# Attention rows of a decoder kernel: both heads scaled on VectorE instead of one on VectorE and one on GpSimd

## The chip, the cores and the metric

One core of a Trainium2 chip runs the whole program. The metric is the device time of one execution in microseconds (us). Before the change the median of 3 runs is 932.4 us (927.18 to 932.52).

## What is computed

One layer of a decoder is run for a prompt of 512 tokens and, with the same weights, for 8 sample sequences of one token each. The part that matters here is the attention of the prompt over its own tokens (selected-block and sliding-window branches). With 512 tokens both branches see all earlier tokens, so each is a causal softmax, and the results are mixed by sigmoid gates:

```python
s_s = jnp.einsum('bqhgd,bhqksd->bhgqks', qg, gk, preferred_element_type=f32) * scale
p_s = masked_softmax(s_s.reshape(sh[:4] + (-1,)), m_s.reshape(...)).reshape(sh)
o_s = jnp.einsum('bhgqks,bhqksd->bqhgd', p_s, gv.astype(f32))
s_w = jnp.einsum('bqhgd,bkhd->bhgqk', qg, kw, preferred_element_type=f32) * scale
p_w = masked_softmax(s_w, (dlt >= 0) & (dlt < WINDOW) & (kpos >= 0)[None, :])
o_w = jnp.einsum('bhgqk,bkhd->bqhgd', p_w, vw.astype(f32))
gt = jax.nn.sigmoid(g.astype(f32)).reshape(B, Tq, NSA_KV_HEADS, NSA_GROUP, 3)
o = gt[..., 0:1] * o_c + gt[..., 1:2] * o_s + gt[..., 2:3] * o_w
```

Everything is fp32. The compressed branch `o_c`, the mLSTM and pool groups, the output projection, the FFN and the samples' own attention belong to the program too; the change touches none of them.

## The kernel before

The kernel has one instruction stream per engine, with semaphores between them that are written out by hand. Its stages run in this order: norms and the input projection (N_IN tiles of weights), mLSTM, the attention loop, the output projection and the FFN. In the dense stages each weight tile is split into a high and a low part: ScalarE writes the high part (line 1043), GpSimd the low part (line 641), TensorE multiplies with both (line 687).

The attention loop works on 32 units, `UNITS = [(hq, i, r) ...]` (line 415): 4 head indices `hq`, for each 4 query blocks `i` of 128 tokens, for each 2 branches `r` (0 selected, 1 window). One unit handles the two heads `hq` and `hq + 4` at once, as `g = 0` and `g = 1`. A unit of query block `i` has rows of (i + 1) x 128 keys, so its width is 128, 256, 384 or 512 per head, and each width comes twice in a row. Eight units make one `hq`. Below, u0 to u7 are the units of one `hq`: u0 and u1 have width 128, u6 and u7 width 512.

For unit k the engines do this:

- TensorE, `scores(k)` (line 907): the scores of both heads into banks 2(k % 2) and the next one. It waits for `p_exp` of unit k - 2, which frees the banks.
- VectorE: adds the causal mask (line 1675) and takes the negative maximum (line 1676, `mx_ready`).
- ScalarE: exponentials with the row sum, once per head (line 1246, `p_exp`), into `pr[k % 3]`.
- VectorE, one iteration later (lines 1684 to 1689): the reciprocal of the sums, times the gate, gives `fac`, one factor for each head. `fac_ready` tells GpSimd. VectorE then multiplies head g = 0's rows by its factor (line 1688, `p_ready`).
- GpSimd (lines 632 to 636): waits for `fac_ready`, multiplies head g = 1's rows by its factor (line 635), and signals `p_pool`.
- TensorE, `flip(k)` three iterations later (line 922): waits for `p_ready` and `p_pool`, and for the copy of the unit before (`pt_act`), then transposes the rows into banks 4 and 5. For r = 0 it also transposes the compressed branch's rows (line 927).
- ScalarE copies the transposed rows to SBUF (line 1239, `pt_act`). VectorE copies the compressed branch's (line 1695, `pt_dve`, r = 0 only).
- TensorE, `values(k)` four iterations later (lines 940 and 943): products with V. For r = 0 it waits for `pt_dve`, and when also i is 0 or 2 it first does `sample_values` (line 957), the value products of one sample sequence, for which that sequence's rows must have come by DMA.
- VectorE evacuates the result (lines 1705 and 1706, after r = 1 units).

TensorE's order within iteration k is `scores(k)`, `flip(k - 3)`, `values(k - 4)`. VectorE's order within iteration k is mask and maximum of unit k, factor and scaling of unit k - 1, the copy for unit k - 3, the evacuation of unit k - 5. Since `fac` has two slots, VectorE waits before it writes the slot of unit v until `p_pool` shows that GpSimd has read it for unit v - 2 (line 1683).

The value rows of the sample sequences are issued meanwhile by SyncE, one page at a time (line 490, 16 per sequence), and one window load per sequence (line 494). GpSimd's part of the loop stands in its program between the second and the third low part of the output weights' tiles; the third waits for a high part that ScalarE makes after the loop.

Of the kernel before, what the change touches and what calls it, by code (L numbers as in the profile page):

```python
# [16 lines left out]
ALU = mybir.AluOpType  # L17
# [3 lines left out]
P = 128  # L21
# [25 lines left out]
N_IN = 21  # L47
# [117 lines left out]
def trunk_kernel(nc, xT, wst, par_d, con_d, hot_d, ltri_d, pt_d, cacheA, cacheV, winK, winV, mC, mst, plst, ffst,  # L165
                 o_y, o_fm, o_vn, o_st, o_snv, o_wk, o_wv, o_C, o_m, o_pool, o_sC, o_sn, o_sm, o_spool, o_ffp, o_ffs):
    with ExitStack() as ctx:
# [3 lines left out]
        def sem(name):  # L171
            return ctx.enter_context(nc.semaphore(name))
# [60 lines left out]
        sn, gN, cout, smr, cst = lay(27464, [1152, 96, 260, 214, 1024])  # L233
        gN = gN.rearrange("p (i n) -> p i n", i=ST)
# [17 lines left out]
        pr = [pr2[:, 0], pr2[:, 1], md.rearrange("p (r n) -> p r n", r=2)]  # L252
# [34 lines left out]
        fac = sb("fac", [P, 2, 2])  # L287
# [76 lines left out]
        csc_done, pcx_ready, pcx_exp, pc_ready = sem("csc_done"), sem("pcx_ready"), sem("pcx_exp"), sem("pc_ready")  # L364
        qk_done, mx_ready, p_exp, p_ready, t_done = sem("qk_done"), sem("mx_ready"), sem("p_exp"), sem("p_ready"), sem("t_done")
        pt_act, pt_dve, pv_done, o_evac = sem("pt_act"), sem("pt_dve"), sem("pv_done"), sem("o_evac")
        fac_ready, p_pool = sem("fac_ready"), sem("p_pool")
        cout_ready = sem("cout_ready")
        pool_ready, pool_mm, side_mix = sem("pool_ready"), sem("pool_mm"), sem("side_mix")
        snew_done, wsc_done, wsc_evac, sgate_moved, sg_exp = (sem("snew_done"), sem("wsc_done"), sem("wsc_evac"),  # L370
# [44 lines left out]
        UNITS = [(hq, i, r) for hq in range(G) for i in range(ST) for r in range(2)]  # L415
# [150 lines left out]
        def _(pool):  # L566
# [59 lines left out]
            for i, g in enumerate(SPLIT):  # L626
                if i == N_IN:
                    pool.wait_ge(con_landed, 16)
                    pool.wait_ge(rec_landed, 32)
                    pool.wait_ge(mmix_ready, 1)  # L630
                    pool_heads()
                if i == N_IN + 2:
                    for v, (hq, b, r) in enumerate(UNITS):
                        pool.wait_ge(fac_ready, v + 1)
                        nc.gpsimd.tensor_scalar(pr[v % 3][:, 1, 0:(b + 1) * P], pr[v % 3][:, 1, 0:(b + 1) * P], fac[:, v % 2, 1:2], None, ALU.mult)\  # L635
                            .then_inc(p_pool, 1)
                if i == 3 or (7 <= i < N_IN):
                    value_products(half)
                    half += 1
                pool.wait_ge(hi_ready, i + 1)  # L640
                nc.gpsimd.tensor_tensor(wR[:, i % 2, 1, :, :], raw[:, g % RAW, :, :], wR[:, i % 2, 0, :, :].bitcast(F32),  # L641
                                        ALU.subtract).then_inc(lo_ready, 1)
# [3 lines left out]
        def _(pe):  # L646
# [141 lines left out]
            for t in range(2):  # L788
                for i in range(ST):
                    last = nc.tensor.transpose(ps[:, 4 + t, i * P:(i + 1) * P], pT[:, T_MK + t, i * P:(i + 1) * P], ident)  # L790
            last.then_inc(kn_T, 1)
            for c, t in enumerate([T_MQ, T_MQ + 1, T_MK, T_MK + 1, T_G]):
                last = nc.tensor.transpose(ps[0:NB, c // 4, (c % 4) * P:(c % 4 + 1) * P], sT[:, t, :], ident)
            last.then_inc(sn_T, 1)
            for i in range(ST):
                last = nc.tensor.transpose(ps[:, 3, i * P:(i + 1) * P], pT[:, T_G, i * P:(i + 1) * P], ident)
# [18 lines left out]
            for c in range(4 * ST):  # L815
                if c in (0, 8):
                    window_scores(c // 8)
                r, i = c // ST, c % ST
                at = (c % 8) * 2 * NCP
                last = mm(ps[:, r // 2, at:at + 2 * NCP], pT[:, r, i * P:(i + 1) * P], kct[:, 64:64 + 2 * NCP],  # L820
                          start=True, stop=True)
# [89 lines left out]
            def flip(u):  # L911
                hq, i, r = UNITS[u]
                pe.wait_ge(p_ready, u + 1)
                pe.wait_ge(p_pool, u + 1)
                if u == 0:
                    pe.wait_ge(pc_ready, 1)
                    pe.wait_ge(side_mix, 1)
                else:
                    pe.wait_ge(pt_act, u)
                for g in range(2):  # L920
                    for c in range(i + 1):
                        last = nc.tensor.transpose(ps[:, 4 + g, c * P:(c + 1) * P], pr[u % 3][:, g, c * P:(c + 1) * P], ident)  # L922
                if r == 0:
                    if u >= 4:
                        pe.wait_ge(o_evac, u // 2 - 1)
                    for g in range(2):
                        last = nc.tensor.transpose(ps[0:NCP, 6 + u // 2 % 2, 256 + g * P:256 + (g + 1) * P],  # L927
                                                   pc[:, (hq + G * g) * ST + i, 0:NCP], ident)
                last.then_inc(t_done, 1)
# [394 lines left out]
        def _(dve):  # L1324
# [3 lines left out]
            def link(ins):  # L1328

                chain[0] += 1  # L1330
                ins.then_inc(dve_step, 1)
                dve.wait_ge(dve_step, chain[0])
# [336 lines left out]
            for k in range(NU + 5):  # L1669
                if k < NU:  # L1670
                    hq, i, r = UNITS[k]
                    two = ps[:, 2 * (k % 2):2 * (k % 2) + 2, :]
                    dve.wait_ge(qk_done, k + 1)
                    d = two[:, :, i * P:(i + 1) * P]
                    link(V.tensor_tensor(d, d, con_("cq").unsqueeze(1).broadcast_to([P, 2, P]), ALU.add))
                    V.tensor_reduce(nmx[:, k % 2, :], two[:, :, 0:(i + 1) * P], AX, ALU.max, negate=True).then_inc(mx_ready, 1)  # L1676
                if 1 <= k <= NU:
                    v = k - 1
                    hq, i, r = UNITS[v]
                    a = v % 2  # L1680
                    dve.wait_ge(p_exp, v + 1)
                    if v >= 2:
                        dve.wait_ge(p_pool, v - 1)
                    link(V.reciprocal(fac[:, a, :], sm[:, a, :]))
                    V.tensor_tensor(fac[:, a, :], fac[:, a, :], gN[:, i, 3 * hq + 1 + r:3 * hq + 14 + r:12], ALU.mult)\  # L1685
                        .then_inc(fac_ready, 1)
                    dve.wait_ge(fac_ready, v + 1)
                    V.tensor_scalar(pr[v % 3][:, 0, 0:(i + 1) * P], pr[v % 3][:, 0, 0:(i + 1) * P], fac[:, a, 0:1], None, ALU.mult)\
                        .then_inc(p_ready, 1)
                if 3 <= k < NU + 3 and not UNITS[k - 3][2]:  # L1690
                    v = k - 3
                    dve.wait_ge(t_done, v + 1)
                    if v >= 2:
                        dve.wait_ge(pv_done, v - 1)
                    V.tensor_copy(pcT[0:NCP, :, :], ps[0:NCP, 6 + v // 2 % 2, 256:256 + 2 * P].rearrange("p (g n) -> p g n", g=2))\
                        .then_inc(pt_dve, 1)
                if k >= 5 and UNITS[k - 5][2]:
                    v = k - 5
                    hq, i, r = UNITS[v]
                    bank = 6 + v // 2 % 2  # L1700
                    dve.wait_ge(pv_done, v + 1)
                    if i % 2 == 0:
                        b = 2 * hq + i // 2
                        dve.wait_ge(spv_done, b + 1)
                        V.tensor_copy(so8[:, b * P:(b + 1) * P], ps[:, bank, P:2 * P])
                    V.tensor_copy(mix[:, hq, i * P:(i + 1) * P], ps[:, bank, 0:P]).then_inc(o_evac, 1)
# [245 lines left out]
```

## Time and profile before

| | us |
|---|---|
| median of 3 runs | 932.4 |
| lowest and highest run | 927.18, 932.52 |
| the profiled execution: its own time | 932.81 |
| the profiled execution: span, first to last instruction | 931.0 |
| TensorE busy in the span | 845.6 |
| VectorE busy | 494.6 |
| ScalarE busy | 348.5 |
| GpSimd busy | 337.8 |

The mean granted clock of TensorE is 0.905 of full speed. The attention loop begins at about 355 us of the span and its last evacuation is at 461.5 us. "Busy" counts only instructions that compute. PE is TensorE's matmuls, PEld its weight loads, DVE VectorE, ACT ScalarE, POOL GpSimd, SPq the DMA issues of SyncE.

### The profile page before, as it was taken

Reading aid. Unit: us, or ns where it says so; the run is one execution under the profiler, and the core shown is the slowest. Engines: PE = TensorE matmul, PEld = TensorE weight load, DVE = VectorE, ACT = ScalarE, POOL = GpSimd, SP = SyncE. Lnnn points to the kernel's source line nnn. Section 1 sums busy time; section 2 is a strip of 40 time slices with the busy share of each in tenths; the row PEclk is TensorE's granted clock in tenths of the full one; section 3 lists DMA queues with packets and bytes.
Section 4 is the critical chain, followed back from the end, with each engine's and each line's share of the span. In section 5 each row is a group of like instructions: output and inputs, shape, how many; then the busy total and the mean of one; then the engine's idle time right before and its main releaser. Section 6 shows DMA issues by size and latency. Waiting matters only on the chain.

```text
span 931.0 us, 19070 instructions
## 1 busy us (share of the span) xinstructions
PE 845.6 (91%) x7555; PEld 750.2 (81%) x7555; DVE 494.6 (53%) x938; ACT 348.5 (37%) x675; POOL 337.8 (36%) x204
## 2 busy tenths in 40 slices
PE   4669999998998688899899699999999999999994
PEld 3458999987556564566699599999999999999994
DVE  0061456565435985667547756666621366667224
ACT  2432222233322133656432355555311355554321
POOL 0133455451000584434324134444344444443440
PEclk9869999999555655999989899999999999999998
DMA  9732788883105772445026123434322333222222
GB/s 346 289 131 73 221 265 261 270 261 129 35 13 179 283 269 41 105 116 154 8 79 254 46 80 114 114 113 115 102 92 91 106 113 121 93 92 90 92 63 92
DMA packets 72438, 128.28 MB, mean 138 GB/s; under 512 B 13652, under 2 KB 48156, under 8 KB 72096
## 3 DMA queue, kind: packets, MB, share of 16 engines
q1 hardware_dynamic: 65664, 109.65, 36.9%
q10 hardware_dynamic: 6656, 17.43, 5.6%
q8 instruction: 60, 0.98, 0.5%
q14 instruction: 26, 0.21, 0.1%
q0 software_dynamic: 32, 0.00, 0.0%
HBM read 121.39 MB, written 9.11 MB: 140 GB/s over the span
## 4 chain that ended last, share of the span: by engine, by line
PE 73%; DVE 13%; SPq 7%; issue 2%; ACT 2%; DMA 1%; POOL 0%; DVEq 0%; ACTq 0%; POOLq 0%
PE ps L687 56%; SPq L490 2%; PE ps L855 2%; PE ps L870 2%; SPq L429 2%; PE ps L744 2%; PE ps L943 1%; PE ps L922 1%; PE ps L907 1%; DVE sq L1354 1%; PE ps L957 1%; SPq L516 1%; DMA arena<-cache_keys 1%; PE ps L737 1%; DVE hR L1362 1%
## 5 line engine op out<-in xcount | busy, mean ns | idle before, releaser
L687 PE MATMUL ps<-hR,wR 128*128 128x260 f32 x3504 | 436.4, 286 | 21.7 <-ACT hR L1051 17.8
L687 PEld LDWEIGHTS ps<-hR,wR 128*128 128x128 f32 x3504 | 429.9, 191 | 27.1 <-issue 19.3
L641 POOL TENSOR_TENSOR wR<-raw,wR 128x1024 fp32r<-128x1024 f32 x95 | 227.7, 2397 | 321.8 <-ACT wR L1043 321.8
L1043 ACT ACTIVATE wR<-raw 128x1024 fp32r<-128x1024 f32 x95 | 100.4, 1058 | 217.8 <-PE ps L687 214.2
L687 PE MATMUL ps<-fR,wR 128*128 128x260 f32 x1056 | 128.1, 283 | 2.2 <-DVE fR L1746 2.0
L687 PEld LDWEIGHTS ps<-fR,wR 128*128 128x128 f32 x1056 | 127.0, 188 | 3.1 <-DVE fR L1746 2.4
L1768 DVE COPY arena<-arena 128x2 f32<-128x2 f32 x44 | 47.1, 1071 | 94.1 <-ACT arena L1301 94.1
L578 POOL TENSOR_TENSOR arena<-arena,par 128x1024 f32<-128x1024 f32 x16 | 33.4, 2089 | 89.8 <-DMA arena<-cache_keys 89.8
L1372 DVE TENSOR_REDUCE arena<-arena 128x64 f32<-128x1024 f32 x16 | 19.5, 1219 | 86.0 <-POOL arena L578 86.0
L1731 DVE TENSOR_TENSOR t<-ps,mod 128x8 f32<-128x8 f32 x24 | 4.0, 166 | 108.8 <-PE ps L687 108.8
L635 POOL TENSOR_SCALAR arena<-arena,fac 128x128 f32<-128x128 f32 (+3 forms) x32 | 40.7, 1274 | 57.2 <-DVE fac L1685 57.1
L1246 ACT ACTIVATE arena<-ps,nmx 128x128 f32<-128x128 f32 (+3 forms) x64 | 33.2, 526 | 13.5 <-DVE nmx L1676 12.8
L1773 DVE SCALAR_TENSOR_TENSOR arena<-arena,par 128x512 f32<-128x512 f32 x44 | 37.1, 844 | 1.6
L1301 ACT ACTIVATE arena<-arena,par 128x520 f32<-128x520 f32 x44 | 36.2, 823 | 1.5
L1239 ACT ACTIVATE arena<-ps 128x256 f32<-128x256 f32 (+3 forms) x32 | 22.5, 704 | 36.0 <-PE ps L927 29.5
L594 POOL MEMSET arena<- 128x15 f32 x2 | 0.2, 110 | 97.5 <-DVE arena L1575 97.5
L1375 DVE TENSOR_TENSOR arena<-arena,par 128x1024 f32<-128x1024 f32 x16 | 35.2, 2202 | 0.0
L1772 DVE SCALAR_TENSOR_TENSOR arena<-arena,par 128x512 f32<-128x512 f32 x44 | 33.1, 752 | 1.6
L907 PE MATMUL ps<-arena 64*128 64x128 f32 (+3 forms) x128 | 27.8, 519 | 3.3 <-ACT arena L1246 3.3
L922 PEld LDWEIGHTS ps<-con,arena 128*128 128x128 f32 x160 | 17.4, 144 | 16.3 <-issue 11.3
L1298 ACT ACTIVATE arena<-ps 128x520 f32<-128x520 f32 x44 | 25.8, 587 | 6.7 <-DVE fR L1746 6.7
L1025 ACT ACTIVATE sq<-x 128x520 f32<-128x520 f32 x22 | 13.9, 638 | 36.8 <-DVE x L1735 28.7
(334 smaller groups left out, 994.6 us busy)
## 6 DMA issues: line engine op xcount, KB each, us to landing
raw<-weights SPq DMA_DIRECT2D x95, 512.0 KB, 3.8
arena<-cache_keys SPq DMA_DIRECT2D x128, 192.0 KB, 3.3
arena<-weights SPq DMA_DIRECT2D x24, 512.0 KB, 10.5
arena<-cache_values SPq DMA_DIRECT2D x128, 64.0 KB, 1.9
arena<-weights ACTq DMA_DIRECT2D x12, 512.0 KB, 5.6
raw<-weights ACTq DMA_DIRECT2D x12, 512.0 KB, 4.8
x<-xT SPq DMA_DIRECT2D x8, 260.0 KB, 6.3
out_y<-x SPq DMA_DIRECT2D x8, 260.0 KB, 2.2
```

The costliest lines, as they stand in the source:

```text
L578: nc.gpsimd.tensor_tensor(tmpv.rearrange("p (a n j) -> p a n j", a=HALF, j=16), pages[:, s, :, 2 * P:3 * P].rearrange("p a (n j) -> p a n ...
L635: nc.gpsimd.tensor_scalar(pr[v % 3][:, 1, 0:(b + 1) * P], pr[v % 3][:, 1, 0:(b + 1) * P], fac[:, v % 2, 1:2], None, ALU.mult)\
L641: nc.gpsimd.tensor_tensor(wR[:, i % 2, 1, :, :], raw[:, g % RAW, :, :], wR[:, i % 2, 0, :, :].bitcast(F32), ALU.subtract).then_inc(lo_read ...
L687: last = mm(ps[:, a + half, 0:TH], wR[:, i % 2, wp, k, :], src[:, hp, j, half * TH:(half + 1) * TH], start=(j == 0 and q == 0), stop=(j == ...
L907: last = mm(ps[:, 2 * (u % 2) + g, 0:n], pT[hr[g], hq, i * P:(i + 1) * P], pT[hr[g], t, 0:n], start=True, stop=True)
L1043: A(wR[:, i % 2, 0, :, :], raw[:, g % RAW, :, :], ACT.Identity).then_inc(hi_ready, 1)
L1246: last = A(pr[k % 3][:, g, 0:n], ps[:, 2 * (k % 2) + g, 0:n], ACT.Exp, bias=nmx[:, k % 2, g:g + 1], accum_out=sm[:, k % 2, g:g + 1])
L1301: A(yab[:, b, :], zb[:, b, 2:T + 2], ACT.Identity, bias=par_("conv_b", t, t + 1), scale=par_("conv_w", 3 * t + 2, 3 * t + 3)).then_inc(y_r ...
L1375: link(V.tensor_tensor(v, v, par_("wpos", 48, 64).unsqueeze(1).unsqueeze(1).broadcast_to([P, HALF, 8, 16]), ALU.mult))
L1768: V.tensor_copy(ffo_p[:, t, :], z[:, S:S + 2])
L1772: link(V.scalar_tensor_tensor(y[:, 0:S], z[:, 1:S + 1], w[1], y[:, 0:S], ALU.mult, ALU.add))
L1773: last = V.scalar_tensor_tensor(y[:, 0:S], z[:, 0:S], w[0], y[:, 0:S], ALU.mult, ALU.add)
```

## The change

GpSimd's multiply of head g = 1 goes. VectorE multiplies both heads' rows, one after the other, and signals `p_ready` with the second. The semaphores `fac_ready` and `p_pool` are gone, with the wait of TensorE in `flip` and the wait of VectorE before it writes `fac`. The wait of VectorE between the factor and the scaling stays, as a link on its own semaphore.

```diff
@@ GpSimd
-                if i == N_IN + 2:
-                    for v, (hq, b, r) in enumerate(UNITS):
-                        pool.wait_ge(fac_ready, v + 1)
-                        nc.gpsimd.tensor_scalar(pr[v % 3][:, 1, 0:(b + 1) * P], pr[v % 3][:, 1, 0:(b + 1) * P], fac[:, v % 2, 1:2], None, ALU.mult)\
-                            .then_inc(p_pool, 1)
@@ TensorE, flip(u)
                 pe.wait_ge(p_ready, u + 1)
-                pe.wait_ge(p_pool, u + 1)
@@ VectorE
                     dve.wait_ge(p_exp, v + 1)
-                    if v >= 2:
-                        dve.wait_ge(p_pool, v - 1)
                     link(V.reciprocal(fac[:, a, :], sm[:, a, :]))
-                    V.tensor_tensor(fac[:, a, :], fac[:, a, :], gN[:, i, 3 * hq + 1 + r:3 * hq + 14 + r:12], ALU.mult)\
-                        .then_inc(fac_ready, 1)
-                    dve.wait_ge(fac_ready, v + 1)
-                    V.tensor_scalar(pr[v % 3][:, 0, 0:(i + 1) * P], pr[v % 3][:, 0, 0:(i + 1) * P], fac[:, a, 0:1], None, ALU.mult)\
-                        .then_inc(p_ready, 1)
+                    link(V.tensor_tensor(fac[:, a, :], fac[:, a, :], gN[:, i, 3 * hq + 1 + r:3 * hq + 14 + r:12], ALU.mult))
+                    for g in range(2):
+                        last = V.tensor_scalar(pr[v % 3][:, g, 0:(i + 1) * P], pr[v % 3][:, g, 0:(i + 1) * P], fac[:, a, g:g + 1],
+                                               None, ALU.mult)
+                    last.then_inc(p_ready, 1)
```

## Rows read from the trace of the kernel before

**Rows 1.** The page: the chain that ended last, share of the span by engine

```profile
PE 73%; DVE 13%; SPq 7%; issue 2%; ACT 2%; DMA 1%; POOL 0%; DVEq 0%; ACTq 0%; POOLq 0%
```

**Rows 2.** Busy time of each engine in stretches of the loop: stretch, length, engines, clock

```profile
355.00:394.60 39.60, 33.17 (x298) 20.40 (x297) 26.66 (x77) 19.67 (x62) 16.24 (x14) 0.82 0.41 79
...
417.57:440.91 23.34, 22.99 (x271) 15.10 (x269) 17.19 (x50) 14.23 (x40) 10.23 (x9) 1.00 0.51 145
```

**Rows 3.** Waits from 354 to 465 us: in total, times, longest

```profile
POOL arena L635 <- DVE fac L1685: 57.1, 28, 5.7
...
DVE ps L1675 <- PE ps L907: 24.7, 19, 4.6
...
PE ps L957 <- DMA arena<-win_values: 3.0, 1, 3.0
```

**Rows 4.** Groups by shape from 354 to 465 us: the scaling instructions

```profile
L635 POOL TENSOR_SCALAR arena<-arena,fac 128x512 f32<-128x512 f32 x8 | 14.7, 1842 | 5.1 <-DVE fac L1685 5.0
...
L1688 DVE TENSOR_SCALAR arena<-arena,fac 128x512 f32<-128x512 f32 x8 | 4.0, 498 | 0.3
...
L1688 DVE TENSOR_SCALAR arena<-arena,fac 128x384 f32<-128x384 f32 x8 | 3.4, 420 | 0.3
...
L1688 DVE TENSOR_SCALAR arena<-arena,fac 128x256 f32<-128x256 f32 x8 | 2.8, 353 | 0.3
...
L1688 DVE TENSOR_SCALAR arena<-arena,fac 128x128 f32<-128x128 f32 x8 | 2.3, 287 | 0.3
```

**Rows 5.** Timeline, third hq, VectorE: start, duration, instruction, idle before it

```profile
421.40 0.43 DVE L1675 TENSOR_TENSOR ps<-ps,con 128x256 f32<-128x256 f32 x1 [1.44 <-PE ps L907]
...
423.12 0.42 DVE L1688 TENSOR_SCALAR arena<-arena,fac 128x384 f32<-128x384 f32 x1
423.46 0.41 DVE L1695 COPY pcT<-ps 31x256 f32<-31x256 f32 x1
...
425.77 0.42 DVE L1688 TENSOR_SCALAR arena<-arena,fac 128x384 f32<-128x384 f32 x1
426.10 0.28 DVE L1705 COPY arena<-ps 128x128 f32<-128x128 f32 x1
...
428.48 0.49 DVE L1688 TENSOR_SCALAR arena<-arena,fac 128x512 f32<-128x512 f32 x1
428.88 0.41 DVE L1695 COPY pcT<-ps 31x256 f32<-31x256 f32 x1
...
432.84 0.43 DVE L1675 TENSOR_TENSOR ps<-ps,con 128x256 f32<-128x256 f32 x1 [1.76 <-PE ps L907]
```

**Rows 6.** Timeline, second and third hq: TensorE around sample_values, ScalarE's last exponential of u6

```profile
406.05 1.30 PE L957 MATMUL ps<-arena 128*32 128x128 f32 x40 [0.35 <-DVE pcT L1695]
...
426.18 0.68 ACT L1246 ACTIVATE arena<-ps,nmx 128x512 f32<-128x512 f32 x1
...
428.19 0.84 PE L922 MATMUL ps<-con,arena 128*128 128x128 f32 x6
429.39 0.38 PE L957 MATMUL ps<-arena 128*32 128x128 f32 x5 [0.35 <-issue]
```

**Rows 7.** Timeline, GpSimd's pair of scalings and VectorE's scaling inside it

```profile
428.54 3.77 POOL L635 TENSOR_SCALAR arena<-arena,fac 128x512 f32<-128x512 f32 x2 [1.24 <-DVE fac L1685]
...
430.39 0.49 DVE L1688 TENSOR_SCALAR arena<-arena,fac 128x512 f32<-128x512 f32 x1
```

**Rows 8.** Timeline, first hq: sample_values, and the window load that it waits for

```profile
379.68 1.30 PE L957 MATMUL ps<-arena 128*32 128x128 f32 x40 [0.21 <-issue]
...
391.51 0.43 SPq L494 DMA_DIRECT2D arena<-win_values  x1
...
394.62 1.30 PE L957 MATMUL ps<-arena 128*32 128x128 f32 x40 [2.99 <-DMA arena<-win_values]
```

**Rows 9.** Timeline, SyncE: window loads of the second and third hq

```profile
402.81 0.43 SPq L494 DMA_DIRECT2D arena<-win_values  x1
...
425.30 0.44 SPq L494 DMA_DIRECT2D arena<-win_values  x1
```

More of the change, by code:

```diff
@@ L366, in trunk_kernel @@
         pt_act, pt_dve, pv_done, o_evac = sem("pt_act"), sem("pt_dve"), sem("pv_done"), sem("o_evac")
-        fac_ready, p_pool = sem("fac_ready"), sem("p_pool")
         cout_ready = sem("cout_ready")
```

## Prediction, written before the changed kernel was run

> **What bounds the kernel now.** I read the page's chain of waits first. TensorE makes up 73% of the chain that ended last, VectorE 13%, GpSimd 0% [rows 1]. So the GpSimd work that the change removes is on no path that sets the end. The only stretch touched is the attention loop, from about 355 to 461.5 us. The table of stretches comes next [rows 2]. In the third hq, 417.57 to 440.91, TensorE is busy for 22.99 of 23.34 us at full clock (granted 1.00, the 2.4 GHz level), VectorE for 17.19, ScalarE for 14.23, GpSimd for 10.23. There the loop is bound by TensorE, with 0.35 us left over. In the first stretch, 355.00 to 394.60, TensorE is busy for 33.17 of 39.60 us, so something else is late.
>
> Then the waits [rows 3]. GpSimd waits for VectorE's factor, 57.1 us in total, and no row shows anybody waiting for GpSimd's scaling. VectorE's scaling has no matmul waiting for it either; where weight loads are put down to it, they overlap with matmuls in flight. VectorE has 24.7 us of idle time before its mask additions, waiting for scores, in 19 of the 32 units. In the other 13 units it doesn't wait: there it is behind. That is where added work can hurt, so the last view is the timeline of one such place.
>
> In the third hq VectorE waits for the last time at 421.40 [rows 5] (mask of u5) and then runs without a break until after 430 us. In between lies its copy for u4, 428.88 to 429.29, and TensorE needs it: its transposes end at 429.03 (428.19 + 0.84), and `sample_values` starts at 429.39 after 0.35 us of nothing [rows 6]. The trace calls that wait "issue"; at the same place of the second hq, 406.05, it names the copy, line 1695, with the same 0.35 us [rows 6]. So once per hq VectorE sets TensorE's pace, at the copy for u4, and it already does so by 0.35 us. The 0.10 us from the copy's end to the matmul is the hand-over. The fourth hq repeats the pattern. VectorE catches up right after: it waits 1.76 us at 432.84 [rows 5], during `sample_values`.
>
> **The change, part by part.**
>
> *GpSimd's 32 multiplies and its hand-overs go.* GpSimd's multiply of a 512-wide row takes 1.84 us [rows 4], from 0.06 us after VectorE's own start. Even the pair that begins at 428.54 is over at 432.31 (428.54 + 3.77) [rows 7], and the transposes that need it come later, since TensorE starts the flip of a unit two iterations after its scaling. Gain on the path: 0. The wait of VectorE for `p_pool` (line 1683) and that of TensorE (line 914) are satisfied when they are reached; their removal is worth nothing visible, from 0 to a few hundredths of a microsecond each, and TensorE's is covered by matmuls in flight. After the loop GpSimd's next instruction waits for a high part that ScalarE makes only then, so it starts no earlier. No DMA and no queue of SyncE is moved.
>
> *VectorE's link.* The wait after the factor existed before (on `fac_ready`); now it is on VectorE's own semaphore. Cost 0.
>
> *VectorE's second multiply.* 32 instructions are added: 8 of each width. Their durations in the kernel before are 0.498, 0.420, 0.353 and 0.287 us [rows 4], 12.5 us in all (8 x 1.558). What one costs VectorE is less, because the next instruction starts before it has ended: from line 1688's start to the next start there are 0.34 us (384 wide, 423.12 to 423.46), 0.33 us (384, 425.77 to 426.10) and 0.40 us (512, 428.48 to 428.88) [rows 5]. Two multiplies in a row don't occur before. The lower bound of one is 0, if it vanished in a wait; the upper bound is the whole duration. I take the distance from start to start, since it is measured on the same instruction.
>
> Most of them are hidden. Of the eight masks of an hq, five have idle time before them (19 waits in 32 units, 24.7 us, 1.3 us each on average [rows 3]); the scalings of u7, u0, u1, u2 and u3 come right ahead of these five, and the added multiply goes into that idle time. What isn't hidden is what lies between the mask of u5 (421.40) and the copy for u4 (428.88): the scalings of u4, u5 and u6, of widths 384, 384 and 512. The copy moves by 0.34 + 0.33 + 0.40 = 1.07 us. TensorE is already waiting there, so `sample_values` moves by the same 1.07 us. A smaller effect lies before it: the copy for u2 at 423.46 moves by 0.34 and delays TensorE by about 0.2 us, but this is part of the same 1.07, since TensorE then only waits less later. The scaling of u7 comes behind the copy and falls into the 1.76 us before 432.84.
>
> Does anything absorb it? What `sample_values` also waits for is the window load. Its load is issued at 402.81 and 425.30 for the second and third hq [rows 9]; the load issued at 391.51 is the one that TensorE waited for, and TensorE starts at 394.62, so such a load takes about 3.0 us [rows 8]. So they land at 405.8 and 428.3, before the copy's end (about 405.95, a hand-over ahead of 406.05, and 429.29), and SyncE's order doesn't depend on VectorE: no absorption. In the first hq it is otherwise. The place is at 379.68, with 0.21 us of wait, and the delay there can be at most 1.07 us. But then TensorE comes to the next `sample_values` and waits 2.99 us for a window load that SyncE could not issue before 391.51, busy as it is with page loads [rows 8]. A delay up to 2.99 us vanishes there. So three of four count: 3 x 1.07 = 3.2 us.
>
> What is late next: with a TensorE wait of 0.35 + 1.07 = 1.4 us per hq, ScalarE's exponentials of u6 move by 0.34 us too. They end at 426.86 now (426.18 + 0.68), and what waits for them are the scores of the next u0, short matmuls just ahead of the transposes at 428.19 [rows 6]; about 0.8 us of room is left, and they stay hidden.
>
> *A rule against the change.* The rows give a scaling of 512 a cost of 0.40 us and one of 384 0.33 us [rows 5]. The Trainium skill, VectorE: DVE Perf Modes, section on the TRN2 errata, says that an SBUF to SBUF instruction pays a fixed 58 cycles besides its elements, so that two short instructions pay it twice where one long one pays it once. By that formula, with two elements a cycle, the three would cost about 0.27 + 0.27 + 0.33 = 0.87 us, an estimate from the page, and the sum would be 2.6 us instead of 3.2. The rows are taken instead.
>
> The sum is made against the profiled execution: 932.81 + 3.2 = 936.0 us. That execution lies 0.4 us above the median of the runs, so against the median I expect 932.4 + 3.2 = 935.6 us, 0.34% more.
>
> **The rivals.**
>
> *Everything exposed (slower by over 1%).* VectorE becomes the bound of the whole loop, not of three units in eight. The place is the mask addition, the price the whole 12.5 us of added duration, the time 932.4 + 12.5 = 944.9. For it: VectorE's 17.19 us per hq become 20.3 (plus 2 x 1.558), and hand-overs between its linked instructions aren't counted as busy. Against it: 24.7 us of idle time before the masks [rows 3], which is twice the added work, and 5 of the 8 units of an hq have such idle time. It decides from the point where the copy of u4 comes so late that VectorE no longer has any wait before 432.84; that needs 1.76 us more than now and 0.4 us at most is added there. Chance 0.07.
>
> *Nothing is exposed.* The second multiply flows behind the first, or the load of the window is what TensorE waits for after all. The margins of 0.2 and 1.0 us between landing and copy, worked out above, are small enough that a load landing 1 us later in another run would swallow the delay. Time 932.4. Chance 0.20.
>
> *VectorE gains from GpSimd's silence.* If the two engines hinder each other at the SBUF, VectorE's instructions get shorter once GpSimd is quiet. Against it: VectorE's scaling at 430.39 runs wholly inside GpSimd's pair and takes 0.49 us, as does the one at 428.48 that starts before GpSimd does [rows 5, 7]. The price would have to come from the rest of VectorE's run from 421.40 to 429.29; if each of its instructions in it were 5% shorter, that is 0.4 us per hq, 1.2 us in all, and the time would be 934.4, or 931.2 where the multiply is hidden too. Chance 0.06. The Trainium skill, GPSIMD Engine Reference, section Key points, says that GpSimd shares its SBUF interfaces with VectorE and that they contend with a VectorE instruction that uses both ports or has two SBUF inputs, which speaks for this rival; the two equal durations speak against its size here.
>
> *The change doesn't do what it says.* A wait that remains (for `p_exp`, `pt_act`) could hold both multiplies where they were. That is the case of no exposure, and is counted there.
>
> **How the numbers follow.** Forecast 0.67, everything exposed 0.07, nothing exposed 0.20, GpSimd's silence 0.06. About 1% is what a measurement of this kernel can tell from no change. The bounds of the unknown cost are 0 and the full durations, 4 x (0.420 + 0.420 + 0.498) = 5.4 us, so 932.4 to 937.8. The runs of the kernel before spread downward by 5 us, which a median of few runs can inherit in part: low end 930.5. The upper end takes in a part of the way to the first rival: 940. Slower by over 1% is above 941.7: 0.07. Faster by over 1% is below 923.1; no case reaches it, and I leave 0.02 for what I haven't seen. The rest, 0.91, is within 1%.
>
> **What would show it.** Right: in the changed trace TensorE waits some 1.4 us before line 957 in the second, third and fourth hq, for line 1695; an hq of the later ones takes 24.4 instead of 23.34 us; the wait for the window load in the first hq shrinks from 2.99 to about 2.2 us, and its end stays at 394.6; two multiplies in a row start 0.33 to 0.41 us apart at widths 384 and 512; VectorE's idle time before its masks falls but doesn't vanish. Wrong: an hq of 23.34 us as before (nothing exposed), or no idle time before the masks and waits of TensorE in most units (everything exposed), or line 1688's instructions shorter than 0.42 and 0.498 us (GpSimd's silence).

## The result and the profile after

The changed kernel takes 933.68 us (median of 20 runs, 930.87 to 938.68), the kernel before 931.85 us (median of 20 runs, 926.64 to 935.92). The ratio is 1.0034, with a 95% interval of 1.0021 to 1.0047: 2.0 to 4.4 us slower, 3.2 us in the middle. The two medians by themselves differ by only 1.8 us, the two means by 3.0 us. The prediction was 935.6 us, a change of +3.2 us or 0.34%.

The page of the changed kernel: busy time of the engines, and the chain that ended last.

```profile
PE 844.9 (91%) x7555; PEld 749.1 (80%) x7555; DVE 501.4 (54%) x970; ACT 348.9 (37%) x675; POOL 297.9 (32%) x172
...
PE 73%; DVE 14%; SPq 7%; issue 2%; ACT 2%; DMA 1%; POOL 0%; DVEq 0%; ACTq 0%; POOLq 0%
```

GpSimd lost 39.9 us of work (337.8 to 297.9), none of which was on the chain [rows 1]. VectorE's share of the chain rose from 13 to 14%. The span of this one execution is 930.7 us, even 0.3 us under that of the kernel before. The timed runs say otherwise; why this one execution doesn't show the cost comes below.

The timeline of VectorE in the third hq of the changed kernel: start, duration, instruction, idle before it. Line 1668 is the mask (1675 before), 1678 the scaling (1688), 1686 the copy (1695), 1696 the first evacuation (1705).

```profile
419.62 0.43 DVE L1668 TENSOR_TENSOR ps<-ps,con 128x256 f32<-128x256 f32 x1 [1.17 <-PE ps L901]
...
421.35 0.75 DVE L1678 TENSOR_SCALAR arena<-arena,fac 128x384 f32<-128x384 f32 x2
422.01 0.41 DVE L1686 COPY pcT<-ps 31x256 f32<-31x256 f32 x1
...
424.32 0.75 DVE L1678 TENSOR_SCALAR arena<-arena,fac 128x384 f32<-128x384 f32 x2
424.99 0.28 DVE L1696 COPY arena<-ps 128x128 f32<-128x128 f32 x1
...
427.37 0.88 DVE L1678 TENSOR_SCALAR arena<-arena,fac 128x512 f32<-128x512 f32 x2
428.17 0.41 DVE L1686 COPY pcT<-ps 31x256 f32<-31x256 f32 x1
...
432.13 0.43 DVE L1668 TENSOR_TENSOR ps<-ps,con 128x256 f32<-128x256 f32 x1 [1.37 <-PE ps L901]
```

From the mask of u5 to the copy for u4 it is 8.55 us (419.62 to 428.17), where it was 7.48 us (421.40 to 428.88) [rows 5]: 1.07 us more. The pairs take 0.66, 0.67 and 0.80 us from start to the next start, twice what one took to within 0.02 us. The idle time before the mask at the other end fell from 1.76 to 1.37 us.

TensorE's first matmul of `sample_values` (line 950, before 957) in the changed kernel, from the first to the third hq, with the idle time before it.

```profile
379.68 1.30 PE L950 MATMUL ps<-arena 128*32 128x128 f32 x40 [0.91 <-issue]
...
391.79 1.30 PE L950 MATMUL ps<-arena 128*32 128x128 f32 x40 [0.16 <-DMA arena<-win_values]
...
404.28 1.30 PE L950 MATMUL ps<-arena 128*32 128x128 f32 x40 [0.91 <-issue]
...
416.16 1.30 PE L950 MATMUL ps<-arena 128*32 128x128 f32 x40
...
428.68 1.30 PE L950 MATMUL ps<-arena 128*32 128x128 f32 x40 [0.91 <-issue]
...
440.56 1.30 PE L950 MATMUL ps<-arena 128*32 128x128 f32 x40
```

This gives the yardstick for all that follows. Call the distance from an hq's first `sample_values` to its second the first interval, and from there to the next hq's the second. In the changed kernel the first interval is 12.49 us (391.79 to 404.28) and 12.52 us (416.16 to 428.68); before it was 11.43 us (394.62 to 406.05 [rows 6, 8]) and 11.46 us (417.93 to 429.39). The second interval is 11.88 us, as before. So each hq pays 1.06 us, all of it in the first interval. Inside one execution these intervals repeat to a few hundredths of a microsecond wherever no window load is late and the granted clock is 1.00, while whole runs spread over 8 us.

The waits of the changed kernel from 371 to 465 us (in total, times, longest) say where TensorE spends it.

```profile
PE ps L950 <- issue: 3.7, 4, 0.9
...
PEld ps L920 <- DVE arena L1697: 0.9, 3, 0.3
...
PE ps L933 <- DVE pcT L1686: 0.5, 3, 0.2
```

Three places share the loss. `sample_values` waits 0.91 us, where it waited 0.35 before. The values of u2 (line 933) wait 0.17 us for VectorE's copy. And the weight load of the transposes of u4's compressed rows (line 920) waits 0.3 us for line 1697, the evacuation of u1. From start to start of TensorE's work these are 0.56, 0.23 and 0.26 us more than before, together the 1.06 us; the prediction put them all in one place.

Why does the profiled execution not show 3.2 us? SyncE's page loads. The timeline of SyncE in the changed kernel:

```profile
365.30 23.31 SPq L489 DMA_DIRECT2D arena<-cache_values  x32
388.65 0.44 SPq L493 DMA_DIRECT2D arena<-win_values  x1
```

and in the kernel before:

```profile
366.04 25.43 SPq L490 DMA_DIRECT2D arena<-cache_values  x32
```

The same 32 issues took 2.1 us less, and began 0.7 us earlier. So the window load that held TensorE until 394.62 before [rows 8] landed 2.8 us earlier here, and TensorE reached it almost when it had landed (0.16 us of wait). That is a difference between executions: in two other kernels of this study with the same SyncE program, a_copy_first and third_slack, the 32 issues took 23.1 and 25.1 us. From the second hq on, the changed trace loses three times 1.06 us against that of before: from the first `sample_values` of the second hq to the last one it is 61.29 us (391.79 to 453.08), and 58.11 us before (394.62 to 452.73). By that point it is 0.35 us behind; what makes the whole span 0.3 us shorter lies after the loop.

### The profile page after: what moved, and what is told of

Read it like the earlier page. It is cut to its first block, busy times and chain, and to the rows that moved or that the text cites. A ratio compares the mean times of both kernels' runs of the same rounds, so it can differ in the third digit from the quotient of the medians.

```text
span 930.7 us, 19039 instructions
## 1 busy us (share of the span) xinstructions
PE 844.9 (91%) x7555; PEld 749.1 (80%) x7555; DVE 501.4 (54%) x970; ACT 348.9 (37%) x675; POOL 297.9 (32%) x172
## 4 chain that ended last, share of the span: by engine, by line
PE 73%; DVE 14%; SPq 7%; issue 2%; ACT 2%; DMA 1%; POOL 0%; DVEq 0%; ACTq 0%; POOLq 0%
PE ps L681 56%; PE ps L849 2%; PE ps L864 2%; SPq L489 2%; SPq L428 2%; PE ps L738 2%; PE ps L936 1%; DVE sq L1347 1%; PE ps L950 1%; SPq L515 1%; PE ps L915 1%; DMA arena<-cache_keys 1%; PE ps L731 1%; PE ps L901 1%; DVE hR L1355 1%
## 5 line engine op out<-in xcount | busy, mean ns | idle before, releaser
L1368 DVE TENSOR_TENSOR arena<-arena,par 128x1024 f32<-128x1024 f32 x16 | 32.8, 2050 | 0.0
L1669 DVE TENSOR_REDUCE nmx<-ps 128x2 f32<-128x256 f32 (+3 forms) x32 | 26.4, 825 | 1.1
```

The costliest lines, as they stand in the source:

```text
L1368: link(V.tensor_tensor(v, v, par_("wpos", 48, 64).unsqueeze(1).unsqueeze(1).broadcast_to([P, HALF, 8, 16]), ALU.mult))
```

## The experiments

**Which of the 32 multiplies cost.** Two kernels divide them. `ONPOOL` lists the units whose head g = 1 stays on GpSimd, with `fac_ready` and `p_pool` for these units alone:

```diff
+        ONPOOL = [v for v in range(len(UNITS)) if v % 8 in (4, 5, 6)]        # wide_on_pool
+        ONPOOL = [v for v in range(len(UNITS)) if v % 8 not in (4, 5, 6)]    # rest_on_pool
...
-                    for g in range(2):
+                    for g in range(1 if v in ONPOOL else 2):
```

> The changed kernel, but head g = 1 of units u4, u5 and u6 of each hq (widths 384, 384, 512) is scaled on GpSimd again; the other 20 units stay on VectorE. Theory (only what lies between the mask of u5 and the copy for u4 counts): from the first to the second sample_values of the second, third and fourth hq 11.4 us as in the kernel before (12.5 in the changed one), TensorE's wait there 0.35 us; time that of the kernel before, 0 +- 1 us, so about 3 us under the changed kernel. Rival (every added multiply costs a little): 20 of 32 multiplies stay, some 1.5 to 2 us of the 3.2 stay, spread over the whole hq, with intervals of 11.7 or more and over 11.95 for the other half.

> The complement: GpSimd scales head g = 1 of u0 to u3 and u7, VectorE both heads of u4, u5 and u6 only. Theory: 12.5 us from the first to the second sample_values as in the changed kernel, other half 11.95; the full 3.2 us over the kernel before. Rival (every multiply counts, or GpSimd's absence gives something back): 1.2 to 1.7 us over the kernel before.

TensorE's `sample_values` in the third hq, first of wide_on_pool:

```profile
412.86 1.30 PE L960 MATMUL ps<-arena 128*32 128x128 f32 x40
...
424.31 1.30 PE L960 MATMUL ps<-arena 128*32 128x128 f32 x40 [0.35 <-DVE pcT L1703]
```

then of rest_on_pool:

```profile
413.22 1.30 PE L960 MATMUL ps<-arena 128*32 128x128 f32 x40
...
425.73 1.30 PE L960 MATMUL ps<-arena 128*32 128x128 f32 x40 [0.91 <-issue]
```

11.45 us with 0.35 us of wait, and 12.51 us with 0.91: the kernel before and the changed kernel, to 0.01 us. The fourth hq agrees (11.43 and 12.52 us). In wide_on_pool's second hq it is 11.58 us, with 0.49 us of wait for a window load. Twelve multiplies carry the whole interval, the other twenty nothing. The times agree: 1.0015 of the kernel before (0.999 to 1.004) and 1.0042 (1.0017 to 1.0067). The first of them can't be told from 1 or from 1.0034 by itself; the intervals in the traces decide.

**More VectorE work, inside the run and outside.** Two kernels add a third multiply, by 1.0, which changes no value:

```diff
+                    if v % 8 in (7, 0, 1, 2, 3):        # third_slack;  third_run: (4, 5, 6)
+                        link(last)
+                        last = V.tensor_scalar(pr[v % 3][:, 1, 0:(i + 1) * P], pr[v % 3][:, 1, 0:(i + 1) * P], con_("ones", 0, 1), None, ALU.mult)
```

> The changed kernel with a third multiply (by 1.0, in place on head g = 1, behind the second, with a wait between) on VectorE in units u7, u0, u1, u2 and u3 of each hq. Added VectorE work start to start about 0.52 + 2 x 0.3 + 2 x 0.38 = 1.9 us per hq, 7.5 us in all. Theory (there is idle time ahead of those masks): intervals 12.5 and 11.95 us as before, at most 0.3 us more per hq where u2's slack of 0.3 us is used up; total 0 to 1 us. Rival (everything VectorE does counts): 1.9 us more per hq, up to 7.5 us in all.

> The changed kernel with a third multiply (by 1.0, in place on head g = 1, behind the second with a wait between) in units u4, u5 and u6 only, between the mask of u5 and the copy for u4. Added start to start: the link lets the second end (0.42 - 0.33 and 0.49 - 0.40, plus 0.04 each), then the third 0.33, 0.33 and 0.40: 0.46 + 0.46 + 0.53 = 1.45 us. Theory: interval 12.5 + 1.45 = 13.9 to 14.0 us, other half 11.9, 4.4 us over the changed kernel from three hqs and up to 5.8 with the first. Compare third_slack, where more VectorE work elsewhere brought 0.18 us per hq. Rival (the chain is not that of VectorE): less than 1 us per hq.

TensorE's `sample_values` in the third hq of third_slack:

```profile
417.34 1.30 PE L950 MATMUL ps<-arena 128*32 128x128 f32 x40
...
429.83 1.30 PE L950 MATMUL ps<-arena 128*32 128x128 f32 x40 [0.91 <-issue]
```

and of third_run:

```profile
420.06 1.30 PE L950 MATMUL ps<-arena 128*32 128x128 f32 x40
...
434.00 1.25 PE L950 MATMUL ps<-arena 128*32 128x128 f32 x37 [1.43 <-issue]
```

The first stays at 12.49 us; its second interval is 12.06 us instead of 11.88 (405.28 to 417.34), so about 1.9 us of added work costs 0.18 us per hq. The second goes to 13.94 us in the third and in the fourth hq, 1.42 us more for an expected 1.45 us of added work. In time: 1.0040 (1.0011 to 1.0069) and, from six runs, 1.0072 (1.0046 to 1.0098).

The second hq of third_run doesn't fit: 16.00 us (392.18 to 408.18). There TensorE had waited 2.09 us for the window load, and behind it the granted clock was 0.50, the lower of TensorE's two levels (1.2 GHz), for some 6 us. Stretch, length, busy time of TensorE, its weight loads, VectorE, ScalarE and GpSimd, then the granted clock:

```profile
394.00:400.00 6.00, 6.00 (x28) 3.03 (x30) 2.45 (x7) 1.13 (x4) 0.00 (x0) 0.50 0.35 97
```

In the kernel before a wait of 2.99 us at the same place left the clock at 1.00, so why it fell here stays open. This execution took 939.92 us, the longest of the six.

**The place of the copy.** The copy for unit k - 3 goes ahead of the factor and scaling of unit k - 1, in both kernels:

```diff
+                if 3 <= k < NU + 3 and not UNITS[k - 3][2]:
...
+                    V.tensor_copy(pcT[0:NCP, :, :], ...).then_inc(pt_dve, 1)
                 if 1 <= k <= NU:
...
-                if 3 <= k < NU + 3 and not UNITS[k - 3][2]:
...
```

> The changed kernel with VectorE's copy for unit k - 3 placed ahead of factor and scaling of unit k - 1 instead of behind them. Theory (the copy for u4 is late because the scaling stands before it): the copy starts 1.2 us earlier (0.19 + 0.19 + 0.40 + 0.40), TensorE's wait before sample_values goes from 0.91 to about 0, the first interval falls from 12.5 to 11.1 to 11.3 us, the time falls by 3.5 to 4 us against the changed kernel, to 0.5 to 1 us under the kernel before. Rival (VectorE's throughput is what bounds the stretch, not the place of the copy): the wait moves to another place, the scores or the transposes, and the interval stays over 12 us.

> The kernel before with the same move of the copy. Theory: the 0.35 us of TensorE's wait before sample_values vanish, the first interval falls from 11.4 to 11.1 us, the time by 1.0 us (three times 0.35). Rival (that wait is the hand-over itself or something else than the copy): 0.35 us stay.

TensorE in the third hq of a_copy_first:

```profile
414.47 1.30 PE L950 MATMUL ps<-arena 128*32 128x128 f32 x40
...
423.83 0.41 PE L920 MATMUL ps<-con,arena 128*31 128x128 f32 x2 [0.31 <-DVE arena L1697]
...
426.00 1.30 PE L950 MATMUL ps<-arena 128*32 128x128 f32 x40
```

The wait before `sample_values` is gone and the interval falls from 12.5 to 11.53 us, less than the expected 11.1 to 11.3: 0.31 us are left at another thing that stands behind the scalings, the evacuation of u1, for which the transposes of u4's compressed rows wait. So the rival, a wait that moves to another place, holds for a small part. The time is 1.0000 of the kernel before (0.998 to 1.002): within that interval, the order of VectorE's instructions wins back the cost of the change.

TensorE in b_copy_first, third hq and start of the fourth:

```profile
412.78 1.30 PE L957 MATMUL ps<-arena 128*32 128x128 f32 x40
...
423.91 1.30 PE L957 MATMUL ps<-arena 128*32 128x128 f32 x40
...
436.47 1.30 PE L957 MATMUL ps<-arena 128*32 128x128 f32 x40 [0.61 <-DMA arena<-win_values]
```

11.13 us, as expected, but TensorE then waits 0.61 us at the next window load. The time, 0.9986 (0.9967 to 1.0006), isn't clear of 1. Against this kernel, which has the copy in the same place, a_copy_first is still 0.40 us slower per hq (11.53 against 11.13 us): the new order doesn't make the added multiplies free.

**What absorbed the first hq's delay.** The window load of sequence 2 is put ahead of the page loads of sequence 3, in both kernels:

```diff
             load_values(2)
+            sp.wait_ge(spv_done, 1)
+            load_window(2)
             load_values(3)
             for b in range(2, NB):
-                sp.wait_ge(spv_done, b - 1)
-                load_window(b)
+                if b > 2:
+                    sp.wait_ge(spv_done, b - 1)
+                    load_window(b)
```

> The changed kernel with the window load of sample sequence 2 issued ahead of the page loads of sequence 3 instead of behind them. Theory (what absorbs the first hq's delay is this load's issue): the wait of TensorE for the window at the beginning of the second hq goes; that sample_values begins at about 391.6 us in all executions, whatever SyncE's page loads take. In traces where the load was late (before: by 2.99 us) this is a gain up to 3 us, in the changed kernel's own trace it was late by 0.16 only. Time 0 to 2 us under the changed kernel. Rival (the load itself or the pages are late): the wait stays or names the pages.

> The kernel before with the same early window load. Theory: without that wait the first hq's delay would count too, so the distance to a_win_early grows from 3.2 to 3.9 us (0.91 - 0.21 = 0.7 more); the second hq's first sample_values begins at about 390.9 us; time 1 to 3 us under the kernel before. Rival (the first hq never had a share): distance 3.2.

In a_win_early, TensorE's `sample_values` of sequence 3 and the window load that it needs:

```profile
399.75 0.43 SPq L493 DMA_DIRECT2D arena<-win_values  x1
...
402.76 1.30 PE L953 MATMUL ps<-arena 128*32 128x128 f32 x40 [1.50 <-ACT arena L1235]
```

and the same matmul in b_win_early:

```profile
402.61 1.30 PE L960 MATMUL ps<-arena 128*32 128x128 f32 x40 [2.12 <-DMA arena<-win_values]
```

The wait at sequence 2 went (its `sample_values` begins at 389.66 and 389.38 us without a wait), and a new one came at sequence 3, in both kernels at the same time, 402.6 to 402.8 us. The trace of a_win_early names ScalarE, but the copy that TensorE needs from it there, that of u4, had ended at 400.27 us; the load was issued at 399.75, and with the 3.0 us that such a load takes to land it is there at about 402.75. So my theory was too narrow. What holds TensorE is not that one load but SyncE's rate: 16 page loads and a window load take it 10 to 14 us with what stands between them, nearly what TensorE needs for one sequence. With the load moved, the delays of the first and of the second hq both vanish in SyncE's lateness, and two hqs are left that count. The traces show these two: from sequence 3 to the last `sample_values` it is 48.79 us in a_win_early and 46.68 us in b_win_early, 2.11 us or 2 x 1.06 apart. The times are 1.0005 (0.9982 to 1.0028) and 0.9978 (0.9959 to 0.9998) of the kernel before; their distance, 0.27% or 2.5 us, is near it, but with intervals of this width it can't exclude the 3.9 us that I had expected.

The trace of a_win_early also shows that the first hq is a case of its own. From 363 to 371 us the granted clock was 1.00 in it, and 0.50 in the traces of before and after. With TensorE that much faster VectorE is further behind: TensorE waits 1.50 us for the copy for u2 and 1.38 us before `sample_values`, where the changed kernel's trace has no wait and 0.91 us.

The window loads can also leave SyncE altogether, since GpSimd is idle in the loop of the changed kernel (this queue counts on semaphores of its own, `vwin_soft`; the edit on SyncE, which drops `load_window` from its loop, and the one on TensorE, which waits for `vwin_soft`, are left out here):

```diff
+                if i == N_IN + 2:
+                    for b in range(2, NB):
+                        pool.wait_ge(spv_done, b - 1)
+                        pool.dma_start(vwin[:, b % 2], winV[:, b]).then_inc(vwin_soft[b % 2], 16)
```

> The changed kernel, with the window loads of sample sequences 2 to 7 issued by GpSimd, which is idle in the loop now, instead of SyncE, behind whose page loads they stand. Theory (the loads are late because SyncE's 16 page loads per sequence take 10 to 14 us and stand before each of them): no wait for a window at any sample_values; the second hq's first one starts at 391.6 us or earlier, intervals 12.5 and 11.9 us throughout; time 0 to 2 us under the changed kernel. Rival (the pages themselves are late): TensorE waits at the same places without the window, 0 us. A danger: GpSimd's DMA goes through another queue and may take longer to land than 3.0 us; it has 20 us.

TensorE in a_pool_windows, second hq:

```profile
391.65 1.30 PE L957 MATMUL ps<-arena 128*32 128x128 f32 x40
...
404.17 1.30 PE L957 MATMUL ps<-arena 128*32 128x128 f32 x40 [0.91 <-issue]
```

No wait for a window is left anywhere, and the intervals are 12.52 and 11.88 us. The pages were in time. The time is 1.0002 (0.9978 to 1.0026), against 1.0034 (1.0021 to 1.0047) of the changed kernel: it points to a gain, but the intervals overlap.

**Does GpSimd's silence matter?** GpSimd makes 32 multiplies of the same widths on other data, which nobody needs:

```diff
+                        pool.wait_ge(fac_ready, v + 1)
+                        link(G.tensor_scalar(sq[:, 0, 0:(b + 1) * P], par[:, 0:(b + 1) * P], con_("ones", 0, 1), None, ALU.mult))
```

> The changed kernel, but GpSimd makes 32 multiplies of the same widths beside VectorE's, released by the same hand-over from the factor, reading parameters and writing a scratch tile; nobody waits for them and their result is not used. Theory (GpSimd's silence brought nothing): all as in the changed kernel, interval 12.5 us, VectorE's 512 wide scaling 0.48 to 0.50 us, 0 +- 1 us. Rival (the two hinder each other at the SBUF, and the change got part of its cost back by GpSimd's silence): VectorE's scalings get longer, the interval passes 12.7, time 0.6 us and more over the changed kernel.

In the decoy kernel, VectorE's scalings of width 512 as a group (mean 700 ns), and in the third hq the second of a pair beside GpSimd's multiply:

```profile
L1685 DVE TENSOR_SCALAR arena<-arena,fac 128x512 f32<-128x512 f32 x16 | 10.5, 700 | 0.3
```

```profile
429.96 1.78 POOL L635 TENSOR_SCALAR sq<-par,con 128x512 f32<-128x512 f32 x1 [1.98 <-DVE fac L1681]
...
430.23 0.92 DVE L1685 TENSOR_SCALAR arena<-arena,fac 128x512 f32<-128x512 f32 x1
```

The same group in the changed kernel, with GpSimd silent:

```profile
L1678 DVE TENSOR_SCALAR arena<-arena,fac 128x512 f32<-128x512 f32 x16 | 7.1, 483 | 0.3
```

My theory fell here. A scaling that begins inside GpSimd's multiply takes 0.92 us, one without it 0.48. The first of the same pair began at 429.82, 0.14 us ahead of GpSimd's multiply, and took 0.49 us. TensorE's `sample_values` of the third hq in the decoy kernel:

```profile
417.98 1.30 PE L955 MATMUL ps<-arena 128*32 128x128 f32 x40
...
431.57 1.30 PE L955 MATMUL ps<-arena 128*32 128x128 f32 x40 [1.35 <-issue]
```

13.59 us, 1.07 more than in the changed kernel and 2.13 more than in the kernel before, and 1.0064 (1.0042 to 1.0086) of it in time. The added multiplies cost twice as much where GpSimd works beside them.

**A version that beats both.** Copy and evacuation both ahead of the scaling, and the window loads on GpSimd. For comparison the kernel before gets the two moves on VectorE (b_frees):

```diff
-                if 1 <= k <= NU:
...
                 if 3 <= k < NU + 3 and not UNITS[k - 3][2]:
...
                 if k >= 5 and UNITS[k - 5][2]:
...
+                if 1 <= k <= NU:
...
```

> The changed kernel with three moves: VectorE's copy for unit k - 3 and its evacuation of unit k - 5 both ahead of factor and scaling of unit k - 1 (with the copy alone, TensorE still waited 0.31 us for the evacuation, line 1697, before line 920), and the window loads on GpSimd. Theory: interval 11.1 to 11.3 us, other half 11.9, no window wait, 1.3 x 3 + 0.9 = 4.8 us and up to 2 us more under the changed kernel; 927 to 929 where the kernel before has 931. Rival (VectorE's throughput holds the stretch): interval stays at 11.5 or above, 3 us under the changed kernel.

> The kernel before with copy and evacuation ahead of factor and scaling. Theory: as with the copy alone (11.0 to 11.1 us), since there TensorE waited for nothing else; it then waits more for windows, as SyncE's page loads can't be faster, so 0 to 1 us under the kernel before. Rival (evacuation first is worth something here too): another 0.2 us or more per hq.

TensorE in the third hq of a_best:

```profile
408.09 1.30 PE L957 MATMUL ps<-arena 128*32 128x128 f32 x40
...
419.42 1.30 PE L957 MATMUL ps<-arena 128*32 128x128 f32 x40 [0.22 <-issue]
```

11.33 us, no wait for a window, 926.48 us in the median, 0.9956 of the kernel before (0.9932 to 0.9981): 4.1 us under it and, by the two ratios, 7 us under the changed kernel. The span of its profiled execution, 921.4 us, overstates it: TensorE's granted clock from 355 to 371 us was 0.89 there and 0.59 to 0.61 in the profiles of before and after, and the same work at the head of the first hq took 3.84 us (361.68 to 365.52) instead of 7.00 (365.07 to 372.07). From the second `sample_values` to the last, the part behind that stretch, a_best's trace takes 69.62 us, that of before 73.05 and that of the changed kernel 73.40. These 3.4 us are most of the 4.1 against the kernel before; of the 7 us against the changed kernel the traces show 3.8 there. b_frees is at 0.9996 (0.9976 to 1.0016), with 11.03 us in the third hq and a window wait of 2.08 us in its second: no gain can be told from its time while SyncE holds the loop. Window loads on GpSimd were not tried in the kernel before, where GpSimd's stream is busy with its waits for the factors. Which part of a_best's gain is due to which of its edits wasn't separated beyond a_copy_first and a_pool_windows.

Each ratio is to the kernel before as timed beside that kernel.

| kernel | first interval, third hq | ratio to before |
|---|---|---|
| before | 11.46 | 1 |
| changed | 12.52 | 1.0034 |
| wide_on_pool | 11.45 | 1.0015 |
| rest_on_pool | 12.51 | 1.0042 |
| third_slack | 12.49 | 1.0040 |
| third_run | 13.94 | 1.0072 |
| a_copy_first | 11.53 | 1.0000 |
| b_copy_first | 11.13 | 0.9986 |
| a_win_early | 12.51 | 1.0005 |
| b_win_early | 11.46 | 0.9978 |
| a_pool_windows | 12.51 | 1.0002 |
| decoy | 13.59 | 1.0064 |
| a_best | 11.33 | 0.9956 |
| b_frees | 11.03 | 0.9996 |

## Why the prediction was right, and where it wasn't

- *GpSimd's work and hand-overs are worth nothing on the path.* Right: wide_on_pool, with both hand-overs for its units, has the interval of the kernel before to 0.02 us in the third and fourth hq.
- *Only the scalings of u4, u5 and u6 are exposed.* Right, and shown from both sides: moved to VectorE alone they give the whole cost, the others alone none; a third multiply there costs its full length, elsewhere a tenth.
- *The price, 0.34 + 0.33 + 0.40 = 1.07 us from start to start.* Right: 8.55 - 7.48 = 1.07 us on VectorE, 1.06 us between TensorE's marks. The Trainium skill, VectorE: DVE Perf Modes, section on the TRN2 errata, led to an estimate of 0.87 us; worked out without rounding up, its formula gives 0.85 us and 2.5 us in all. The trace gives 1.07. At both widths the rows lie 0.07 us above the formula (0.33 against 0.26, 0.40 against 0.33), so it is its fixed part that is too small here and not its part per element. The same section says itself that the formula comes out too short for a single instruction.
- *TensorE's wait grows to 1.4 us in one place.* The sum was right, the place half: 0.91 us stand before `sample_values`, the rest at two earlier places, one of which waits for an evacuation that I had not looked at. a_copy_first ran into the same evacuation.
- *The first hq's delay is absorbed by the late window load, whose wait shrinks to 2.2 us and ends at 394.6.* Right that this load absorbs it: in the changed kernel's trace TensorE came 0.16 us before the load had landed, so without the first hq's delay it would only have waited longer. Wrong in its numbers: the wait was 0.16 us and ended at 391.79, since SyncE began 0.7 us earlier and its issues took 2.1 us less. The prediction took SyncE's times of one execution for fixed.
- *Three of four hqs count.* Right in the two profiled executions, not proved for the timed runs. SyncE's first 32 issues vary by almost 3 us from execution to execution, and its later loads come close too: taking 3.0 us to land, the window loads of sequences 3, 4 and 5 were there an estimated 0.2, 0.5 and 1.1 us ahead of TensorE in the kernel before, and 1.1 to 1.8 us in the changed one. With another timing on SyncE fewer hqs can count, as the two of a_win_early show, or perhaps all four; no run shows how often. The measured 2.0 to 4.4 us holds 2 x 1.07 and 4 x 1.07 alike. That three fits its middle is not proof of three, and that the ratio came out at just 1.0034 is luck.
- *GpSimd's silence brings nothing.* Right as a number, for a wrong reason. I took two equal durations, one of them "wholly inside GpSimd's pair", as evidence that the engines don't hinder each other. In fact VectorE's scaling at 430.39 began 1.85 us after the pair's start, just when one of GpSimd's multiplies (1.84 us each [rows 4]) ended and the next began [rows 7]. Each of VectorE's scalings in the kernel before began with one of GpSimd's, 0.06 us ahead of it in these rows. A multiply that begins so isn't hindered in the decoy kernel either (0.49 us); one that begins 0.27 us after GpSimd's is. Why the first kind escapes, no run shows. The change removed the neighbour together with adding the work, so its second multiplies ran clean, and the price per multiply that I had read from such clean rows held. The Trainium skill, GPSIMD Engine Reference, Key points, says that the two contend where a VectorE instruction uses both ports or has two SBUF inputs. The trace of the decoy kernel agrees that they contend, 0.92 against 0.48 us; it doesn't show ports.
- *Everything exposed* fell: 16.6 us of idle time before the masks are left of 24.7 [rows 3]. *Nothing is exposed* fell as well: three intervals are 12.5 us and not 11.4.

## What to carry to other kernels

Where work is moved onto an engine with idle time, find the stretches in which that engine does not wait, and count only what lands between its last wait and the next result that somebody is already waiting for. The cheapest repair is often not to move the work back but to let that result pass in front of it: here the copy ahead of the scaling brought the time back to that of the kernel before. And when a gain or a loss on one engine goes missing, look at the queue that runs at nearly the same pace; here SyncE's page loads took up part of what TensorE won or lost.

## What the runs showed of the hardware that I had not expected

VectorE's fp32 multiply of 128 x 512 elements in SBUF takes 0.48 us alone and 0.92 us inside a multiply of GpSimd, while GpSimd's own took 1.78 us, not longer than the 1.84 us of its multiply in the kernel before [rows 4]; no run shows the decoy's multiply alone. VectorE's copies out of PSUM and its reductions of PSUM stayed as they were beside GpSimd (406 and 1224 ns in the changed and in the decoy kernel). A pair of VectorE multiplies costs twice the start-to-start distance of one, to 0.02 us. The same 32 page loads take SyncE 22.9 (decoy) to 25.6 us (third_run) to issue, by execution, with no difference in SyncE's program. TensorE's granted clock fell to 0.50 for some 6 us behind a wait of 2.09 us in third_run, and stayed at 1.00 behind one of 2.99 us in the kernel before.
